# An encoder layer in split float32r products: every SBUF tile placed at a multiple of 64 bytes in place of 32

## What is computed

```python
h = rmsnorm(x, g_mix_pre)
q_a, k_a, v_a, q_r, k_r, v_r, g_r, gate_a, gate_r = split_in(h @ w_in)
o_a = sliding-window attention with sinks (8 heads, 2 key heads of 64)
o_r = retention in chunks (4 heads, keys of 128, values of 256), group norm, * silu(g_r)
merged = sigmoid(gate_a) * (o_a @ w_branch_attn) + sigmoid(gate_r) * (o_r @ w_branch_ret)
x = x + rmsnorm(merged @ w_out, g_mix_post)
h = rmsnorm(x, g_ffn_pre)
x = x + rmsnorm((silu(h @ w_ffn_gate) * (h @ w_ffn_up)) @ w_ffn_down, g_ffn_post)
x = x + (p @ w_ple_proj) * sigmoid(x @ w_ple_gate)
```

## Time and profile before

| | |
|---|---|
| median of 3 runs | 1014.32 us (1013.77 to 1015.25) |
| the profiled execution's own time | 1015.18 us |
| its span, first to last instruction | 1013.5 us |
| TensorE matmuls, busy | 992.2 us, 98% of the span, 7220 instructions |
| weight loads, busy | 960.9 us, 95% |
| VectorE | 632.5 us, 62% |
| ScalarE | 399.7 us, 39% |
| GpSimd | 85.8 us, 8% |
| mean granted TensorE clock | 0.996 |

### The profile page before, as it was taken

One profiled execution on the slowest core, in us unless ns is written; L12 is line 12 of the kernel. 1 busy time (PEld: TensorE's weight loads), 2 busy tenths in 40 slices (PEclk: granted clock), 3 DMA queues, 4 the chain that ended last, 5 costly groups with the idle time before them and its releaser, 6 DMA issues.

```text
span 1013.5 us, 19083 instructions
## 1 busy us (share of the span) xinstructions
PE 992.2 (98%) x7220; PEld 960.9 (95%) x7220; DVE 632.5 (62%) x1244; ACT 399.7 (39%) x693; POOL 85.8 (8%) x140
## 2 busy tenths in 40 slices
PE   6999999999999999999999899999999999999997
PEld 5999989898999999999999899999999999999997
DVE  5545665766666643434548789724997369965762
ACT  4324433423343522222544455423454135443252
POOL 1022212112110000000001200000000000030000
PEclk9999999999999999999999999999999999999999
DMA  7434212212221222244702513521234213365211
GB/s 206 125 111 128 80 55 64 63 53 67 68 65 56 65 87 83 72 126 132 220 22 84 215 55 94 158 83 43 84 101 129 84 43 114 89 225 155 84 46 49
DMA packets 166197, 98.45 MB, mean 97 GB/s; under 512 B 14656, under 2 KB 162528, under 8 KB 165872
## 3 DMA queue, kind: packets, MB, share of 16 engines
q1 hardware_dynamic: 159904, 79.19, 27.6%
q0 software_dynamic: 4336, 16.67, 4.6%
q10 hardware_dynamic: 1888, 1.64, 0.5%
HBM read 86.79 MB, written 10.75 MB: 96 GB/s over the span
## 4 chain that ended last, share of the span: by engine, by line
PE 91%; DVE 4%; issue 2%; ACT 2%; DMA 1%; DVEq 0%; SPq 0%; ACTq 0%
PE acc L679 34%; PE acc L935 10%; PE acc L937 10%; PE acc L936 10%; PE small L935 6%; PE small L936 6%; PE small L937 6%; PE small L807 2%; PE small L822 2%; PE small L850 1%; PE small L854 1%; PE small L759 1%; PE small L852 1%; PE small L1088 1%; DMA x_row<-in_x_sample 1%
## 5 line engine op out<-in xcount | busy, mean ns | idle before, releaser
L679 PE MATMUL acc<-xh,whi 128*128 128x288 f32 x736 | 163.1, 303 | 1.6 <-DVE wlo L1599 1.5
L679 PE MATMUL acc<-xl,whi 128*128 128x288 f32 x736 | 157.4, 295 | 0.0
L679 PE MATMUL acc<-xh,wlo 128*128 128x288 f32 x736 | 157.1, 294 | 0.0
L1116 ACT ACTIVATE whi<-raw 128x1024 fp32r<-128x1024 f32 (+1 forms) x62 | 62.1, 1001 | 198.3 <-PE acc L679 198.3
L1599 DVE TENSOR_TENSOR wlo<-raw,whi 128x1024 fp32r<-128x1024 f32 (+1 forms) x64 | 74.3, 1162 | 81.1 <-ACT whi L1116 77.8
L679 PEld LDWEIGHTS acc<-xh,whi 128*128 128x128 f32 x736 | 116.8, 189 | 8.5 <-issue 7.4
L679 PEld LDWEIGHTS acc<-xh,wlo 128*128 128x128 f32 x736 | 118.1, 188 | 0.0
L679 PEld LDWEIGHTS acc<-xl,whi 128*128 128x128 f32 x736 | 118.0, 188 | 0.0
L1906 DVE TENSOR_TENSOR wlo<-raw,whi 128x512 fp32r<-128x512 f32 (+2 forms) x93 | 81.0, 872 | 49.6 <-ACT whi L1327 33.8
L935 PE MATMUL acc<-yh,whi 128*128 128x288 f32 x360 | 107.2, 298 | 1.3 <-DVE wlo L1906 1.3
L937 PE MATMUL acc<-yh,wlo 128*128 128x288 f32 x360 | 106.1, 295 | 0.0
(11 more groups left out here) (312 smaller groups left out, 2376.9 us busy)
## 6 DMA issues: line engine op xcount, KB each, us to landing
raw<-in_w_in SPq DMA_DIRECT2D x92, 256.0 KB, 3.2
raw<-in_w_ffn_gate SPq DMA_DIRECT2D x44, 256.0 KB, 3.4
raw<-in_w_ffn_up SPq DMA_DIRECT2D x44, 256.0 KB, 4.0
raw<-in_w_ffn_down SPq DMA_DIRECT2D x32, 256.0 KB, 3.6
res<-x_scratch POOLq DMA_DIRECT2D x16, 288.0 KB, 4.3
raw<-in_w_branch_ret SPq DMA_DIRECT2D x16, 256.0 KB, 2.9
raw<-in_w_out SPq DMA_DIRECT2D x16, 256.0 KB, 4.4
raw<-in_w_ffn_down SPq DMA_DIRECT2D x16, 192.0 KB, 3.6
```

The source lines that it names most:

```text
L679: ins = nc.tensor.matmul(acc[:, a, hf, 0:HALF], w[:, s, at:at + P], x(k)[:, hf * HALF:(hf + 1) * HALF], start=first and n == 0 and m == 0, ...
L1116: nc.scalar.activation(whi[:, s, 0:n], raw[:, s, 0:n], ACT.Copy).then_inc(hi_ready, 1)
```

## The change

The cursor is rounded up to 64 bytes in place of 32, and split_at is rounded down to 64 in place of 32. No instruction, no order and no size changes: the rows of every engine's queue are the same before and after.

```diff
             if at is None:
                 at = cursor[0]
-                cursor[0] += (size + 31) // 32 * 32
+                cursor[0] += (size + 63) // 64 * 64
...
-        split_at = (nc.sbuf_usable_end - 3 * slab) // 32 * 32
+        split_at = (nc.sbuf_usable_end - 3 * slab) // 64 * 64
```

## The result

The changed kernel took 1016.93 us (median of 20 runs, 1014.71 to 1017.93), the kernel before 1014.46 us beside it (20 runs, 1013.33 to 1016.96): ratio 1.0022, 95% interval 1.0016 to 1.0029. It is slower by some 0.2%: the ratio is worth 2.2 us, and the medians differ by 2.5 us. The profiled execution took 1015.95 us, 0.8 us more than that of before.

What follows compares the result with a forecast made beforehand. The prediction took the kernel to be bound by TensorE's stream of matmuls. Its sum was the profiled 1015.18 us + 0, with the time put at the median, 1014.3 us (own range 1012.3 to 1016.3); the stated range was 970 to 1021.

Steps and rivals of the forecast that it cites:

- What bounds the kernel: Whole kernel: a stream of matmuls, TensorE busy 992.2 of 1013.5 us, no stage waiting on others to any extent.
- the slower rival: float32r matmuls on TensorE: operand and weight reads meet when level; 1025 us if all take 133.8 ns, half 1020; chance 0.18.
- the sum's own range for no change: Whole kernel: time stays at the median, 1014.3 us, between 1012.3 and 1016.3; chance 0.45.
- (1): VectorE and ScalarE additions and evictions: same time aligned or not (457 and 458 ns, 406 and 406), taken as nothing.
- (2): DMA loads: at most 0.4 us gain at the head, where TensorE waits for the first x; left out of the sum.
- (3): Weight loads, transposes and float32 matmuls: 0 to 3 ns on 632 matmuls, at most 2 us; taken as nothing.
- (4): The 6588 float32r matmuls of 288 columns: between 59 us less and 11 us more; taken as nothing.
- the third rival: float32r matmuls: TensorE's two read streams might meet when level, spreading rh's pattern; up to 1025 us, chance 0.18.
- The first rival: float32r matmuls: operands fetched in 64-byte pieces, so alignment saves up to 44 us; 974 us, between 955 and 990; chance 0.25.
- The 12 ns over the columns: float32r matmuls of 288 columns at full clock: about 132 ns apart, against 120 ns at one column per cycle.
- What would show each step: Stretch 590 to 660 us: 530 matmuls if unchanged, 558 at 125.4 ns, 523 at 133.8; whole-program mean under 131.8 or over 132.4 refutes.

Runs made afterwards that it cites:

- the change's second profile: The changed kernel run again unaltered, beside the kernel before: 1015.95 us against 1014.90, ratio 1.0012 (1.0003 to 1.0021).
- the second one of before: Profile of the kernel before, nothing changed, compared against itself: 1014.71 us against 1014.64, ratio 1.0004 (0.9995 to 1.0013).
- the one-half table: Distances from a kernel computing no layer: TensorE stretches on one half of a slab, moving operand 0 to 224 bytes past the weights; no time or ratio given.

## Why the prediction was wrong

**What bounds the kernel** held: TensorE 993.8 of 1014.3 us, and what was found of the loss is in its matmuls. The measured 1016.93 us lies inside the stated range of 970 to 1021, in the part that was kept for the slower rival; the sum's own range for no change, 1012.3 to 1016.3, missed it by 0.6 us. That the number came so near is not the merit of the account: the loss was small because only some of the matmuls moved to a slower place, which the prediction had not worked out.

**(1) VectorE and ScalarE at nothing** held. The additions of 288 columns, aligned both times for sqacc and now for yt and res too (busy us, mean ns), answer to the earlier trace rows:

```profile
L2265 DVE TENSOR_TENSOR yt<-yt,res 128x288 f32<-128x288 f32 x16 | 7.3, 458 | 0.6
L2212 DVE TENSOR_TENSOR sqacc<-sqacc,sq_out 128x288 f32<-128x288 f32 x14 | 6.4, 456 | 5.6 <-ACT sq_out L1530 5.6
```

**(2) DMAs at most 0.4 us at the head.** The head of the profile was 1.2 us shorter. By the same matching it was 1.8 us shorter in the change's second profile, 0.3 in the second one of before, 1.4 with everything 32 past (64 up), and 0.8 us longer with the slabs 96 up. It goes with the execution, not with the remainder by 64.

**(3) Transposes and float32 matmuls at nothing** held: the transposes of line 873 are 109 ns apart in both profiles, the float32 matmuls of 256 columns of line 807 215 ns.

**(4) "I take nothing" for the 6588 float32r matmuls is the step that failed**, with its second reason: three distances with one remainder by 64 did show that something else is at work, but I took that as a ground for no change, although the same edit also changed that something else. It is the difference between the two operands' places. The prediction said of the six small tiles, which take 384 bytes in place of 192, that "they do not alter this". By 64 bytes that is right; but they are the reason why the slabs moved up by 224 bytes and the weights ahead of them by only 32, a shift of 192 against each other, which is 64 by 128. The front part listed xh at 32 and whi at 96 by 256 before, 0 and 128 after; the third rival said that the two streams might meet when they start level, and the loss is of its kind: 132.17 became 132.65 ns to 372 us, where the bulk of the matmuls read xh. Its size was well over what came: not 133.8 for all 6588 (11 us), but 0.5 ns on 1861 and 0.1 ns or less on most of the others, 1.3 us by the sum, and 2.2 and 1.2 measured. Level is 133.3 where it stays in the slow pattern (1.15 ns on the first half would have been 2.1 us); four stretches of it fell into the pattern near 130, and in most others the first dozen matmuls ran closer together than the pattern they settled in. The timeline of the changed kernel in one of them (stretch of 118):

```profile
48.87 0.42 PE L679 MATMUL acc<-xl,whi 128*128 128x288 f32 x2
...
50.43 0.42 PE L679 MATMUL acc<-xl,whi 128*128 128x288 f32 x2
```

12 matmuls in 1.56 us, 130.0 ns. In the feed-forward the second weight buffer stood level with the slabs before and after. With the first one the difference of yh and fh went from 192 to 128 bytes for one half of the rows and from 64 to 0 for the other. By the one-half table (133.4 and 132.2 ns, 133.3 and 131.65) that would be a small gain; the mean went up by 0.08 ns, from 132.59 to 132.67. So the table gives the size there, next to nothing, but not the sign.

My bound for the rival, "from 0.3 ns per matmul on" for 2 us, was sound as arithmetic. Its chance was held down to 0.18 by the sentence that rh's fastest pattern speaks against position, and that sentence was wrong: slow and fast pattern are the two states of one level pair.

**The first rival (64-byte fetches)** is refuted for 288 columns: with everything 32 past (64 up) the first half ran at 132.13 ns, with everything aligned at 132.65. The 12 ns over the columns are there in both. My comparison with the Trainium skill's page "TensorE: Matmul & The Clock Gate", section "Back-to-back issue gap", had less to say than I made of it: the section gives that formula for a matmul by itself, and other figures for a stream in which each matmul has its weight load, which is what runs here. By the Trainium skill's page "SBUF — State Buffer", section "Specifications (TRN2)", with lines of 16 bytes, 32 and 64 would be the same; as to a tile's own place the runs agree. They do not show the line: 4 bytes off cost 136.6 ns, 8 bytes 133.3 and 16 bytes 132.8 in the one stretch each that tried it.

**What would show each step**: 529 matmuls from 590 to 660 us looked like no change, since that window reads yh, th and fh and none of xh. The mean over the whole program, the other sign that I named (over 132.4), was already at 132.5 in the profile of before by the table above. I had taken 132.1 from the count of one stretch of 70 us, and that count holds 2 matmuls that only reach into the window: 528 start in it, 132.6 ns apart. The half clock's distance stayed at 240 ns, as it should (answering to the earlier trace rows):

```profile
939.02 0.44 PE L935 MATMUL acc<-fh,whi 128*128 128x288 f32 x1
939.26 0.44 PE L936 MATMUL acc<-fl,whi 128*128 128x288 f32 x1
```

**Left open.** How much of the 2.2 us of the first comparison is the distances: the second gave 1.2 and the sum 1.3, and the lower granted clock of the changed kernel's runs was not told apart. What starts a level stretch in its fast pattern. Whether it is the read of the weights that collides with the moving stream; the runs show that their difference in place and the order of the addresses matter, not the mechanism inside.

## What to carry to other kernels

A change of alignment moves every tile against every other, so list the pairs of operands that one instruction reads together before and after, and look at their differences, not at each tile's own remainder. When a distance shows several patterns with equal code, that is a hidden variable, and the edit has to be asked whether it moves it. In a kernel with TensorE busy 98% of the time, 0.5 ns on a good quarter of its matmuls (0.9 us) is near the limit of what a comparison of 20 runs can tell; a small kernel with one stretch for each pair of places gave the table in a single execution. Such a table holds for its own width and order of matmuls: at 256 and 512 columns the best place was another one, and in the feed-forward loop it did not hold everywhere.

## What the runs showed of the hardware

- The distance between float32r matmuls of 288 columns at the full clock depended on the difference of their two operands' places: 130.0 to 134.4 ns at multiples of 32 bytes, 136.6 ns at 4 bytes. With ScalarE, VectorE and the queues idle it ran from 131.6 to 134.4 ns at multiples of 32 bytes. At 256 and 512 columns 64 apart was slower than level (117.8 against 116.6 ns, 231.1 against 230.0).
- Level pairs had two steady patterns, 129 and 131 ns in turn or about 131, 131, 132, 140; one and the same kernel showed both at one place in two executions (130.0 and 133.3 ns near 454 us).
- At the half clock no such effect showed: the matmuls of 288 columns lay 240 ns apart in every placement.
